# A second half of weights asked for later, gate rows moved behind features, and unread products on TensorE, in a routed mixture-of-experts layer

## The reference, cut to what matters

```python
def ec_ffn(h, w_router, w1, w3, w2):
    b, n, d = h.shape
    cap = EC_CAPACITY * n // N_EXPERTS          # 128 sample tokens, 16 prompt tokens for each expert
    logits = jnp.einsum('bnd,de->bne', h, w_router).astype(jnp.float32)
    aff = jax.nn.softmax(logits, axis=-1).transpose(0, 2, 1)
    gate, idx = lax.top_k(aff, cap)
    xs = jax.vmap(lambda hb, ib: hb[ib])(h, idx)
    hid = jax.nn.silu(jnp.einsum('becd,edf->becf', xs, w1)) * jnp.einsum('becd,edf->becf', xs, w3)
    y = jnp.einsum('becf,efd->becd', hid, w2) * gate[..., None].astype(h.dtype)
    return jax.vmap(lambda ib, yb: jnp.zeros((n, d), yb.dtype).at[ib.reshape(-1)].add(yb.reshape(-1, d)))(idx, y)
```

## Time and profile before

| | us |
|---|---|
| median of 3 runs (1598.79 to 1604.21) | 1600.95 |
| the profiled execution | 1600.96 |
| its span, from the first to the last instruction | 1598.8 |
| TensorE busy in the span | 1551.1 (97%) |
| VectorE, ScalarE, GpSimd busy | 562.4, 420.2, 105.7 |

### The profile page before, as it was taken

The page is one execution under the profiler, slowest core; times in us unless marked ns, Lnnn a source line. Parts: engine busy times, 40 slices in busy tenths (PEclk is TensorE's granted clock), DMA queues, the critical chain, the costliest instruction groups (busy, mean ns, idle before and its releaser), DMA issues.

```text
span 1598.8 us, 26689 instructions
## 1 busy us (share of the span) xinstructions
PE 1551.1 (97%) x10773; PEld 1249.3 (78%) x10773; DVE 562.4 (35%) x1343; ACT 420.2 (26%) x958; POOL 105.7 (7%) x108
## 2 busy tenths in 40 slices
PE   5999999999999999999799999999999999999997
PEld 3744545766766666544599999999999999999996
DVE  2201545765656574126674111111111111111114
ACT  4300112555545453234311111101111111111114
POOL 0005300000000000111000000000000000000000
PEclk9999999999999999999899999999999999999999
DMA  9780002000010300352476787778787787877776
GB/s 381 271 292 33 30 7 59 8 20 8 0 26 0 125 1 1 129 187 80 185 269 234 277 312 252 268 274 306 268 296 266 266 299 267 310 252 270 270 235 248
DMA packets 120922, 291.06 MB, mean 182 GB/s; under 512 B 17503, under 2 KB 21126, under 8 KB 117918
## 3 DMA queue, kind: packets, MB, share of 16 engines
q1 hardware_dynamic: 115534, 270.80, 46.7%
q0 software_dynamic: 4752, 17.30, 4.1%
q10 hardware_dynamic: 576, 2.10, 0.3%
HBM read 266.18 MB, written 21.64 MB: 180 GB/s over the span
## 4 chain that ended last, share of the span: by engine, by line
PE 93%; DVE 3%; DMA 2%; ACT 1%; issue 1%; SPq 0%; DVEq 0%; POOLq 0%; ACTq 0%
PE ps L1163 31%; PE ps L1192 16%; PE ps L805 9%; PE ps L601 9%; PE ps L906 7%; PE ps L854 5%; PE ps L839 4%; PE ps L671 2%; PE ps L759 2%; DMA wreg<-in_w_ada_dram 1%; PE ps L771 1%; PE ps L784 1%; PE ps L621 1%; PE ps L1112 1%; PE ps L1120 1%
## 5 line engine op out<-in xcount | busy, mean ns | idle before, releaser
L1163 PE MATMUL ps<-mreg,wreg 128*128 128x144 f32 x4096 | 517.1, 286 | 1.4 <-ACT hreg L1455 1.4
L1163 PEld LDWEIGHTS ps<-mreg,wreg 128*128 128x128 f32 x4096 | 508.8, 190 | 1.8 <-ACT hreg L1455 1.6
L1192 PE MATMUL ps<-mreg,wreg 128*128 128x144 f32 x2048 | 267.3, 287 | 0.5 <-DVE mreg L2118 0.5
L1192 PEld LDWEIGHTS ps<-mreg,wreg 128*128 128x128 f32 x2048 | 259.5, 191 | 0.7 <-DVE mreg L2118 0.7
L2105 DVE TENSOR_TENSOR mreg<-ps,mreg 128x144 f32<-128x144 f32 x120 | 36.9, 307 | 434.2 <-PE ps L1163 434.1
L805 PE MATMUL ps<-wreg 128*128 128x512 f32 (+2 forms) x400 | 171.7, 519 | 0.2
L1483 ACT ACTIVATE mreg<-ps 128x144 f32<-128x144 f32 x128 | 37.1, 290 | 444.7 <-PE ps L1163 444.7
L601 PE MATMUL ps<-hreg,wreg 128*128 128x512 f32 (+1 forms) x432 | 142.9, 489 | 0.0
L906 PE MATMUL ps<-wreg,mreg 128*128 128x512 f32 x288 | 130.8, 598 | 0.0
L839 PEld LDWEIGHTS ps<-const,hreg 128*128 128x128 f32 x648 | 79.9, 141 | 58.8 <-issue 39.3
L601 PEld LDWEIGHTS ps<-hreg,wreg 128*128 128x128 f32 x432 | 70.5, 191 | 69.7 <-issue 69.4
(11 more groups left out here) (280 smaller groups left out, 1124.5 us busy)
## 6 DMA issues: line engine op xcount, KB each, us to landing
wreg<-in_w_e_dram SPq DMA_DIRECT2D x96, 2048.0 KB, 12.0
wreg<-in_w_ada_dram SPq DMA_DIRECT2D x24, 1024.0 KB, 10.0
out_dram<-wreg SPq DMA_DIRECT2D x9, 512.0 KB, 2.6
wreg<-in_x_sample_dram SPq DMA_DIRECT2D x8, 512.0 KB, 5.0
wreg<-in_w_out_dram SPq DMA_DIRECT2D x1, 4096.0 KB, 12.8
x_rows<-wreg SPq DMA_DIRECT2D x8, 512.0 KB, 4.2
xn_rows<-wreg SPq DMA_DIRECT2D x8, 512.0 KB, 2.6
wreg<-x_rows SPq DMA_DIRECT2D x8, 512.0 KB, 9.3
```

The lines of the kernel that those rows point to most:

```text
L1163: mm = pe.matmul(o[:, 0:CAP], w[s][:, k, (f % 4) * P:(f % 4 + 1) * P], xsT[b][:, k, :], start=(k == 0), stop=(k == KD - 1))
L1192: mm = pe.matmul(bank[4 + dm % 2][:, 0:CAP], w2[f // 4][:, f % 4, dm * P:(dm + 1) * P], hidT[:, f, :], start=(f == 0), stop=(f == 7))
```

## The change

On SyncE the two requests for `w1[1]` and `w3[1]` move behind the wait for `rows_in[0]`. `prompt_rows` keeps only the two products of the index rows; the two of the gate rows become `prompt_gate_rows`, which TensorE runs after feature 5 and the last block of `gathered`, with a third count on `row_mm`. VectorE's `prompt_gates` moves behind its six last blocks of `gathered` and waits for that count. TensorE gets 17 products of the identity with itself into PSUM bank 2, which nothing reads: six before `prompt_by_expert` (behind a wait for the last eviction of a projection, `o_out`), five after it, two before `prompt_rows`, four behind the wait for `xp_ok` ahead of the first expert.

```diff
-            sp.wait_ge(o_mm, 2 * NT)
-            first_weights(w1, w_e1, w1_in, 1)
-            first_weights(w3, w_e3, w3_in, 1)
             for s in range(2):
                 sp.wait_ge(x2_st[s], 16 * 4)
                 sp.wait_ge(xn_st[s], 16 * 4)
+            sp.wait_ge(o_mm, 2 * NT)
             sp.wait_ge(rows_in[0], 16)
+            first_weights(w1, w_e1, w1_in, 1)
+            first_weights(w3, w_e3, w3_in, 1)
...
+            def unread_products(b, n):
+
+                for _ in range(n):
+                    pe.matmul(bank[b][:, 0:P], ident, ident, start=True, stop=True)
...
                 for half in range(2):
                     if half:
                         pe.wait_ge(aff_out, 2)
-                    for a, x in enumerate((diag_idx, diag_gate)):
-                        mm = pe.matmul(bank[ROWS_BANK[half]][:, a * P:(a + 1) * P], ones[0:NE, :],
-                                       x[0:NE, half * P:(half + 1) * P], start=True, stop=True)
-                    mm.then_inc(row_mm, 1)
+                    pe.matmul(bank[ROWS_BANK[half]][:, 0:P], ones[0:NE, :], diag_idx[0:NE, half * P:(half + 1) * P],
+                              start=True, stop=True).then_inc(row_mm, 1)
+
+            def prompt_gate_rows():
+                pe.wait_ge(onehot_ok, 2)
+                for half in range(2):
+                    mm = pe.matmul(bank[ROWS_BANK[half]][:, P:2 * P], ones[0:NE, :],
+                                   diag_gate[0:NE, half * P:(half + 1) * P], start=True, stop=True)
+                mm.then_inc(row_mm, 1)
...
             by_token(8)
+            pe.wait_ge(o_out, 2 * NT)
+            unread_products(2, 6)
             prompt_by_expert()
+            unread_products(2, 5)
...
                 gathered(0, 0, k, k, first=True)
+            unread_products(2, 2)
             prompt_rows()
             for k in range(KD):
                 prompt_features(0, k)
                 if k < 6:
                     gathered(0, 0, k + 2, k + 2, first=True)
+                if k == 5:
+                    prompt_gate_rows()
             pe.wait_ge(xp_ok, 1)
+            unread_products(2, 4)
             pe.wait_ge(gated_ok, 2)
             expert(0, 0, first=True)
...
                     dve.wait_ge(onehot_ok, half + 1)
+                    dve.wait_ge(row_mm, 3)
                     dve.tensor_tensor(pick_gate[:, cols], pick_p[:, cols], bank[ROWS_BANK[half]][:, P:2 * P],
...
             prompt_picks()
-            prompt_gates()
...
             for k in range(2, KD):
                 gathered(0, k, k)
+            prompt_gates()
```

## The result

The changed kernel takes 1629.51 us (median of 4 runs, 1628.40 to 1631.61) against 1602.58 for the kernel before (4 runs): a ratio of 1.0172, interval 1.0151 to 1.0192. It is slower by 1.7%, where 0.3% faster was forecast. The profiled execution took 1631.61 with a span of 1629.7, so 30.9 us more span than before.

What follows compares the result with a forecast made beforehand. TensorE's chain was taken as the bound, held at routing's end by expert 0's gather and a half-speed clock. First product at 785.0, not 789.93, saves 4.9 us from 1600.95: 1596.0, range 1593.0 to 1600.0.

Steps and rivals of the forecast that it cites:

- Nothing I see gives it back: After the first expert's earlier start, nothing later was expected to take back the 4.9 us gained.
- The sum: First expert's first product at 785.0 instead of 789.93, 4.9 us gained, so 1596.0 us.
- the slower one: Rival at the first expert's step 4: second weight halves land too late; about 1609 us at 40 us landing; chance 0.06.
- Gather alone, 4.3 us: Expert 0's row gather, with SyncE's loads behind it, lands at 777.2 instead of 780.88, in 4.3 us, not 8.0.
- the rival in which the loads did it no harm: Expert 0's gather still lands at 780.9, features 2.55 us later than forecast, 1598.6; 0.11 for all cases of gather gaining less.
- the smaller price: Under queues taking turns, loads cost expert 0's gather only 1.3 us: 1597.1; 0.11 for all cases of gather gaining less.
- Diagonals late next; spread rows at 778.8, features at 779.95: At routing's end, VectorE's diagonals, ready at 778.74, set the pace; features start at 779.95 against 783.60.
- Products hidden ahead of the features: Unread products before the features (six, five, two) fit inside TensorE's waits: 1.3, 1.1 and about 0.7 us, warm.
- Clock held all the way: From 774 to 790 TensorE's granted clock stays 1.00, features end at 783.3, first expert's first product comes at 785.0.
- VectorE's moved gates, cost 0: VectorE's two gate multiplications behind the last gathered block are done by 783.4; later work has slack, cost 0.
- Second halves of weights hidden: `w1[1]` and `w3[1]`, requested about 777.5, land by about 796, before step 4 needs them beyond 804; cost 0.
- Second clock fall, 0 of 0 to 1.7 gained: Behind the token lists' stall, TensorE's slow 3.81 us may vanish, gaining 0 to 1.7 us; 0 taken.

Runs made afterwards that it cites:

- sp_only: Kernel before with SyncE's new request order alone, no gate move or unread products: 1597.97 us, ratio 0.9976.
- A: Not a run: time from expert 0's list (its first 128 x 2 product) to the end of the first expert's first step; 24.30 us before, 21.35 after.
- sp_wide: Kernel before with SyncE's new order and eight unread products of 256 columns, gate rows left in place: 1595.74 us, ratio 0.9958.
- sp_gates: Changed kernel without its 17 unread products, keeping SyncE's new order and the gates' move: 1602.82 us, ratio 1.0003.
- B: Not a run: time from the end of the first expert's first step to the third expert's request for `w2`; 104.36 us before, 104.12 after.
- before_50: Kernel before with 50 already met wait instructions behind TensorE's first product: 1644.34 us (one execution).
- before_67: Kernel before with 67 already met wait instructions at the start of TensorE's program: 1637.20 us, ratio 1.0217.

## Why the prediction was wrong

The step that failed is "Nothing I see gives it back". The sum priced every added instruction by its own time on TensorE and had no term for its place in the program. That term is 32.7 us: five jumps back of the loop, 20.4 us of standing still in all and 12.3 in the steps behind them, in the one shown at a clock of 0.61. None of the rivals was this: the slower one had the second halves of weights landing late, and they landed in time (from 786 on TensorE waits for no DMA). The trace of before held the sign, though not the size: 44 packets in all and none from 1060 to 1500 say that the loop is held whole, and that more code ahead of it may matter.

The Trainium skill ("Runtime: NRT & Kernel Launch", "Instruction fetch mechanics") has the mechanism: TensorE's instruction memory has room for 2048, filled in 16 KiB blocks of 256, and a taken branch to code that isn't there stalls until it is fetched. The packets of 16 KB and the stall at each jump back agree. It also says that only two blocks are kept; the 440 us of before without a packet, with turns of 1666 instructions, do not agree with that.

The other steps, in the order of the forecast:

- **Gather alone, 4.3 us.** Right: 4.3 in the trace after, and sp_only gains 2.9 us of A by SyncE's order alone. (In the price of the rival in which the loads did it no harm, 2.55 should be 2.4, from 778.5 to 780.9.) The loads cost it 3.7 us, where a turn of each queue would have cost 1.3 by the prediction. The rule of the Trainium skill ("DMA: Bandwidth & Descriptors", "Queues, rings and completion order") that spoke for the smaller price, read as an equal share for each queue, doesn't fit these rows.
- **Diagonals late next; spread rows at 778.8, features at 779.95.** Right: features at 779.77.
- **Products hidden ahead of the features.** Right in time: they fill waits, and the features start on time with the clock at 1.00 from 770 on.
- **Clock held all the way.** Half right. It held to 784.55, then fell in the four products (1.62 instead of 0.9) and for part of the first step (5.12 instead of 4.16). The first product of the expert came at 786.17 instead of 785.0: 0.4 from the features' end (783.7 for 783.3), 0.7 from the four. With the first step's 1.0 more, 4.9 less 2.1 is 2.8; A is 2.95 shorter. With wide products the clock held.
- **VectorE's moved gates, cost 0.** True of VectorE. TensorE's half of that move, the gate rows' products, was counted at 0.44 and took 0.64; that is now between features and expert, and 0.2 is gained ahead (features 9.83 behind the list in after, 10.05 in sp_wide). What had no price is the move at the lower clock: without products, in sp_gates, it costs 3.1 us of A.
- **Second halves of weights hidden.** Right. (777.5 and 16 are 793.5 and not the 796 of the sum, which leaves the cover larger still.)
- **Second clock fall, 0 of 0 to 1.7 gained.** Right for this kernel: 0.57 behind the stall of the lists, where the earlier trace rows have 0.55. Its price was right too: B is 1.4 to 1.9 shorter where it stays away.

Open are five things. Which starts of the loop are borne, and by what rule. Why the clock held into the expert with eight wide products and not with seventeen narrow ones that fill about the same time: the profiles show that it did, not why. Why the jumps of before_50 cost 5.0 us at most and those of before_67 4.2. What decides on the clock's second fall. And where between 34 and 50 instructions the edge lies.

## What to carry to other kernels

Where a hot loop's code just fits, any instruction added ahead of it can cost more than the edit can bring: look for instruction packets while the loop runs, and price an edit by the place it gives the loop as well as by its own time. When an edit is slower far from where it was made and at equal steps, put as many instructions that do nothing into the old kernel before looking for a cause in the edit's meaning. Filler that is to keep TensorE busy took half the instructions here when it was made of few wide products.

## What the runs showed of the hardware

- A jump back to code that isn't held costs 4.1 us of TensorE standing still on average in after and before_67 and 4.9 in before_50, nine packets of 16 KB, and in after another 2.5 behind it.
- The loss comes and goes with the place of the loop: 0, 31, 34, 130 + 67 and 217 more instructions ahead of it leave 44 packets, 50 and 67 make 89.
- An instruction of two waits that are already met takes TensorE about 0.11 us (217 in 24.2 us).
- The granted clock stayed at 1.00 from 780.19 to 789.50 with six of eight wide products run ahead of the features (sp_wide), and was 0.65 from 780.82 to 787.02, the features and the wait behind them, without products (sp_only).
